# Column blocks of 512, 512 and 128 instead of 3 x 384 in the attention projections and the output projection of the last tiles

## Chip, cores and metric

One Trainium2 chip, one of its cores. The metric is the device time of one execution in microseconds (us). TensorE (PE) multiplies, VectorE (DVE) and ScalarE (ACT) work on vectors, GpSimd (POOL) does small copies and starts some of the transfers, SyncE (SP) starts the others. Each engine runs its own list of instructions in order; they meet through semaphores.

## What is computed

A two-layer encoder step for a prompt of 1024 tokens and eight samples of 16 tokens, so 1152 tokens in all, with a model width of 1024. What the change touches is, in each layer, the projection before attention and the one behind it:

```python
qa, ka, va, qb, kb, vb = split_even(h @ w_in)      # layer 0, 2304 output columns
y = jnp.concatenate([oa.reshape(b, t, A_WIDTH), ob], axis=-1) @ w_out
...
q, k, v = [z.reshape(b, t, C_HEADS, HEAD_DIM) for z in jnp.split(h @ w_in, 3, axis=-1)]   # layer 1
return o @ w_out, (k_new, v_new)
```

Around them stand a normalisation with shift and scale from a condition vector, a gated residual addition, and behind each attention a gated ConvFFN. All is float32.

## The kernel before

**Layout.** Activations lie transposed: 128 features on the partitions, 1152 tokens as columns; `h` and `hl` hold eight such feature tiles (`KT` = 8). float32 precision is had by splitting each operand into a high part (fp32r) and a low part (bf16): `mm3` (lines 84 to 88) runs three matmuls into the same accumulator, high x high, high x low and low x high, each with its own weight load.

**Stages.** `setup`, then attention "AB" (layer 0), FFN 0, attention "C" (layer 1), FFN 1, `finish`. An attention goes through tiles of 128 output features: A has tiles 0 to 3, B tiles 4 to 7, C tiles 8 to 15. For each tile a `q`, and mostly a `k` and a `v`, is needed, a *tensor* of 128 x 1152, which takes 8 weight tiles (k) times the 1152 columns. B shares a k and v between two tiles, so AB has 20 tensors and C 24.

**The column blocks.** 1152 columns don't fit in one PSUM bank (512 floats), so a tensor is made in three blocks, each over all k. `THIRDS` (line 38) makes them 384 wide. A step `("F", name, b, k)` is one `mm3` of block b (line 1520), `("P", n, b, k)` the same for the output projection of feature block n (line 1556). FFN and the very last projection use `COLS` (line 37) instead: `mm9` (lines 90 to 113) and the FFN's `first_pair` (lines 737 to 753).

**The order of work.** All engines follow one list of steps, made by `tile_steps` (line 1007) for a tile and `first_steps` (line 1067) for the first tensors. In a tile's list stand the attention's steps (`S` scores, `T` transposes of the probabilities, `V` product with the values, `N` and `O` norm and transpose of the output, `K`, `SK`, `VH`, `VI`, `PV` for the cached keys and values of the samples), and between them whole numbers, the slots: places with a weight where projection steps for the *next* tile are put as filler. A slot gets so many steps that the share of steps sent is the share of weights seen. In C with all three tensors a slot holds mostly 2 or 3 `F` steps, with up to 6 in a row near the samples' part. In the last tile of each attention (`last`), where there is no next tile, the filler is the output projection over seven of the eight feature tiles (the eighth is this tile's own output); its 8 x 3 x 7 steps stand in slots of up to 16. The seven earlier tiles' outputs have been spilled to DRAM and are read back into `h` and `hl` before it.

**Banks.** Blocks go in turn to PSUM banks 0 and 1. Block i waits (`f_free`, and line 1553 for `P`) until block i - 2 has been copied out: by ScalarE into `F[name]` for `F` (line 1786), by VectorE's `out_third` (lines 2102 to 2120) for `P`, which adds gate x product to `xT`. Columns from 1024 on are samples with a gate each, so they take two instructions of their own (lines 2115 and 2119). In `first_steps` q and k use six banks at once.

**First tensors.** `first_steps` interleaves q and k row by row of k; blocks 0 and 1 of row k run when VectorE has made row k of `hl` (`mod_dve`), block 2, which holds the samples, four rows later (`LAG`). Then v follows in three blocks, after the ring slot of q's weights has been refilled and split (`W`: ScalarE line 177, VectorE line 182).

**End.** Behind the last tile's steps `mm9` adds the product with the last feature tile, and VectorE's `residual` the result.

Of the kernel before, what the change touches and what calls it, by code (L numbers as in the profile page):

```python
# [14 lines left out]
P = 128  # L15
D = 1024
KT = D // P
SEQ = 1024
NB = 8
NS = 16  # L20
TS = NB * NS
TOK = SEQ + TS
# [12 lines left out]
IN_EVEN = 2304  # L35
THETA = 10000.0
COLS = ((0, 512), (512, 1024), (1024, TOK))
THIRDS = ((0, 384), (384, 768), (768, TOK))


C_ID = 0
# [965 lines left out]
def tile_steps(kind, T, fill, last, nxt):  # L1007


    keys = new_kv(kind, T)  # L1010
    body = []
    lead, early = (0, 0) if last else (6, 4)
    late = 0 if fill == "q" else 1
    for u in range(QB + 1):


        scored = u < QB

        one, two = ([0], [0]) if last and u < 3 else ([4], [4])
        body += [("FA", u - 1)] if u else []  # L1020
        first, second = [("S", u, 0)] if scored else [("QZ", 0)], [("S", u, 1)] if scored else []
        body += first + second + ([("V", u - 2)] if u > 1 else [])
        if u == 0:
            body += [("VT",), ("KT",), ("VS",), lead, ("KR",)] if keys else [lead]
        turned = [("T", u - 1, p) for p in range(pieces(kind, u - 1))] if u else []
        body += ([("N", u - 2)] if u > 1 else []) + one + turned[0:2]
        body += ([("O", u - 2)] if u > 1 else []) + two + turned[2:]
    body += [("LB",), ("V", QB - 1)]
    for g in range(2):
        u, x = QB + g, late if g else 1  # L1030
        body += [("K", g, 0), ("K", g, 1), 3 * x, ("N", u - 1), ("SK", g, 0), ("K", g, 2), ("O", u - 1), 2 * x,
                 ("SK", g, 1), ("K", g, 3), ("SK", g, 2), x, ("SK", g, 3), ("VH", g, 0), ("VH", g, 1), ("X", u), 9 * x,
                 ("FA", u), ("VI", g, 0), ("VI", g, 1)] + ([("QZ", 1)] if g == 0 else []) + \
                [("T", u, 0), 4 * x] + ([("CQ",) + nxt] if g and nxt else []) + \
                [("PV", g, 0), ("VH", g, 2), ("VI", g, 2), ("PV", g, 1), ("VH", g, 3),
                 ("VI", g, 3), ("PV", g, 2), x, ("PV", g, 3), ("V", u)]
    body += ([("CK",) + nxt] if nxt and new_kv(*nxt) else []) + [4 * late, ("N", QB + 1), 4 * late, ("O", QB + 1)]
    total = sum(s for s in body if isinstance(s, int))
    todo = [("P", n, b, k) for n in range(KT) for b in range(3) for k in range(KT - 1)] if last else \
        [("F", name, b, k) for name in fill for b in range(3) for k in range(KT)]  # L1040
    seen = sent = 0
    turn, later, steps = [], [], []
    for s in body:
        if not isinstance(s, int):
            steps.append(s)
            continue
        seen += s
        upto = -(-len(todo) * seen // total)
        if upto > sent or sent == len(todo):
            steps += turn  # L1050
            turn, later = later, []
        steps += todo[sent:upto]
        for f in todo[sent:upto]:
            if unit_ends(f):
                turn += [("W",)]
                later += [("R", f[1])] if f[1] in ("q", "k") else []
        sent = upto
    assert sent == len(todo)
    return steps + turn + later
# [35 lines left out]
def attention(nc, S, G, ins, outs, kinds):  # L1095
    ctx = ExitStack()
    with ctx:
# [7 lines left out]
        q, ql = sb("q", [P, TOK], F32R), sb("ql", [P, TOK], BF16)  # L1105
# [13 lines left out]
        rtmp = sb("rtmp", [P, 2, TS]) if odd else E[:, 1792:2048].rearrange("p (j t) -> p j t", j=2)  # L1119
# [10 lines left out]
        ps, h, hl, K, mb = G.psum, G.h, G.hl, G.consts, G.maskb  # L1130
# [4 lines left out]
        a = m  # L1135
        tiles, total = plan(kinds)
# [367 lines left out]
        def _(pe):  # L1504
            spread_pe(pe, S, G, m, F["v"], rs, rs_s)

            def do(what, kind, T, s, c, turns):
                n = kv(kind, T)
                first = isinstance(T, int) and T == T0
                if what == "F":  # L1510
                    nk, nT = next_tile(kind, T)
                    name, b, k = s[1:]
                    if T == T0 - 1:
                        c = cb + "qkv".index(name)
# [2 lines left out]
                        f_free(kind, T, name, b, n)  # L1517
                    if T == T0 - 1 and name != "v" and b == 0:
                        h_ready(pe, S, m, k)
                    lo, hi = THIRDS[b]  # L1520
                    mm = mm3(pe, ps[:, f_bank(T, name, b), 0:hi - lo], w[:, k * P:(k + 1) * P], wl[:, k * P:(k + 1) * P],
                             h[:, k, lo:hi], hl[:, k, lo:hi], k == 0, k == KT - 1)
                    if k == KT - 1:
# [20 lines left out]
                elif what == "P":  # L1544
                    j, b, k = s[1:]
# [7 lines left out]
                        pe.wait_ge(S.out_evac, 4 * KT * odd + i - 1)  # L1553
                    elif i == 0 and k == KT - 2:
                        pe.wait_ge(S.restored, gone + 32 * 7)
                    lo, hi = THIRDS[b]
                    mm = mm3(pe, ps[:, i % 2, 0:hi - lo], w[:, k * P:(k + 1) * P], wl[:, k * P:(k + 1) * P],
                             h[:, k, lo:hi], hl[:, k, lo:hi], k == 0, k == KT - 2)
                    if k == KT - 2:
# [3 lines left out]
                elif what == "K":  # L1563
                    g, b = s[1:]
# [9 lines left out]
                elif what == "SK":  # L1574
                    g, b = s[1:]
# [14 lines left out]
                elif what == "T":  # L1590
                    u, p = s[1:]
# [15 lines left out]
                    else:  # L1607
                        nb = width(kind, u) // P
                        for i in range(4 * p, min(4 * p + 4, nb if kind == "A" else 2 * nb)):
                            y = e_at(kind, u, i // nb) + i % nb * P  # L1610
                            mm = pe.transpose(dst[:, (i - 4 * p) * P:(i - 4 * p + 1) * P], E[:, y:y + P], ident)
                    mm.then_inc(S.turned, 1)
                elif what == "V" and s[1] < QB:
# [8 lines left out]
                    for j in range(nb):  # L1622
                        x, y = slice(j * P, (j + 1) * P), slice((k0 + j) * P, (k0 + j + 1) * P)
# [11 lines left out]
                elif what == "PV":  # L1635
                    g, b = s[1:]
# [10 lines left out]
                    for j in range(nc_):  # L1647
                        x = slice(j * all_ + b * rows, j * all_ + (b + 1) * rows)
# [101 lines left out]
        def _(act):  # L1750
# [12 lines left out]
            def do(what, kind, T, s, c, turns):  # L1763
                n = kv(kind, T)
                first = isinstance(T, int) and T == T0
                if what == "F" and s[3] == KT - 1:
                    nk, nT = next_tile(kind, T)
                    name, b = s[1:3]
                    if T == T0 - 1:
                        c = cb + "qkv".index(name)  # L1770
# [5 lines left out]
                    if T != T0 - 1 and b == 0:  # L1776
# [5 lines left out]
                            act.wait_ge(S.k_turned, n + 1)  # L1782
                        else:
                            act.wait_ge(S.v_turned, n + 1)
                    lo, hi = THIRDS[b]
                    act.copy(F[name][:, lo:hi], ps[:, f_bank(T, name, b), 0:hi - lo]).then_inc(f_sem[name], 1)
                elif what == "W":
                    split()
                elif what in ("CQ", "CK"):
                    isq = what == "CQ"  # L1790
                    kind, T = s[1:]
                    n = kv(kind, T)
# [31 lines left out]
                elif what == "T":  # L1824
                    u, p = s[1:]
# [6 lines left out]
                elif what == "K":  # L1832
                    g, b = s[1:]
# [98 lines left out]
        def _(dve):  # L1932
# [11 lines left out]
            def do(what, kind, T, s, c, turns):  # L1944
# [4 lines left out]
                elif what == "R" and not odd:  # L1949
                    rotate(s[1], *next_tile(kind, T))  # L1950
                elif what == "P" and s[3] == KT - 2:
                    out_third(s[1], s[2], c)
                elif what == "CQ":
                    dve.wait_ge(S.q_high, s[2] + 1)
                    dve.tensor_tensor(ql[:, :], F["q"][:, :], q[:, :].bitcast(F32), ALU.subtract).then_inc(S.q_low, 1)
# [143 lines left out]
                    dve.tensor_scalar(x, x, rc[:, 0:1], G.cfac[:, 0:1] if kind == "A" else None,  # L2099
                                      ALU.mult, ALU.mult if kind == "A" else ALU.bypass).then_inc(S.probs, 1)  # L2100

            def out_third(n, b, c):

                lo, hi = THIRDS[b]
                if b == 2:
                    ring.done(dve, c)
                else:
                    dve.wait_ge(S.out_ready, (3 * KT - 1) * odd + 2 * n + b + 1)
                upto = min(hi, SEQ)
                y, x = ps[:, (3 * n + b) % 2, 0:hi - lo], G.xT[:, n, lo:upto]  # L2110
                i_ = dve.scalar_tensor_tensor(out=x, in0=y[:, 0:upto - lo], scalar=G.mod[:, a, 16 + n, 0:1], in1=x,
                                              op0=ALU.mult, op1=ALU.add)
                if b == 2:
                    tmp, x = rtmp[:, n % 2, :], G.xT[:, n, SEQ:TOK]
                    ch.then(dve.tensor_tensor(tmp.rearrange("p (b q) -> p b q", b=NB),
                                              y[:, SEQ - lo:hi - lo].rearrange("p (b q) -> p b q", b=NB),
                                              G.mod[:, a, 16 + n, 1:NC9].unsqueeze(2).broadcast_to([P, NB, NS]),
                                              ALU.mult))
                    i_ = dve.tensor_tensor(x, x, tmp, ALU.add)
                i_.then_inc(S.out_evac, 1)  # L2120
# [199 lines left out]
```

## Time and profile before

| what | value |
|---|---|
| three timed runs | 3976.79, 3984.57, 3977.92 us; median 3977.92 |
| profiled execution | 3989.37 us, of which the span from first to last instruction 3987.8 us |
| granted TensorE clock, mean | 0.924 |
| PE matmuls busy | 3534.9 us |
| DVE busy | 2122.8 us |
| ACT busy | 1352.4 us |

The profile lists instructions with start and duration. A matmul's start is stamped when it may begin to enter, and its end is modelled, so durations of neighbours overlap: the pace is read from start to start. PEld are the weight loads. Names read `output<-inputs`. The granted clock is 1.00 at 2.4 GHz and 0.50 at 1.2 GHz. The FFN stages are not touched.

### The profile page before, as it was taken

Reading aid. Unit: us, or ns where it says so; the run is one execution under the profiler, and the core shown is the slowest. Engines: PE = TensorE matmul, PEld = TensorE weight load, DVE = VectorE, ACT = ScalarE, POOL = GpSimd, SP = SyncE. Lnnn points to the kernel's source line nnn. Section 1 sums busy time; section 2 is a strip of 40 time slices with the busy share of each in tenths; the row PEclk is TensorE's granted clock in tenths of the full one; section 3 lists DMA queues with packets and bytes.
Section 4 is the critical chain, followed back from the end, with each engine's and each line's share of the span. In section 5 each row is a group of like instructions: output and inputs, shape, how many; then the busy total and the mean of one; then the engine's idle time right before and its main releaser. Section 6 shows DMA issues by size and latency. Waiting matters only on the chain. (4 is left out here: it accounts for less than half of the span.)

```text
span 3987.8 us, 54257 instructions
## 1 busy us (share of the span) xinstructions
PE 3534.9 (89%) x20953; PEld 2087.5 (52%) x20953; DVE 2122.8 (53%) x3554; ACT 1352.4 (34%) x2665; POOL 485.6 (12%) x1018
## 2 busy tenths in 40 slices
PE   6878788877699999999988888888879999999997
PEld 3545455544464555555545555555546455555554
DVE  5654444455446555555555545545545655555555
ACT  6633444344223222122134444444432322212212
POOL 1012212222110000000010222211201000000000
PEclk8887888778799999999989999988989999999998
DMA  9722222211302111111111333333241211111111
GB/s 348 256 63 75 55 60 78 67 45 48 111 24 60 43 43 38 48 40 41 41 62 48 118 116 113 118 107 99 92 136 43 60 43 43 38 48 39 42 40 57
DMA packets 222127, 303.87 MB, mean 76 GB/s; under 512 B 24339, under 2 KB 174151, under 8 KB 221314
## 3 DMA queue, kind: packets, MB, share of 16 engines
q1 hardware_dynamic: 191938, 190.39, 14.7%
q0 software_dynamic: 30016, 111.15, 9.3%
q8 instruction: 112, 1.84, 0.2%
q14 instruction: 61, 0.50, 0.0%
HBM read 264.76 MB, written 63.95 MB: 82 GB/s over the span
## 5 line engine op out<-in xcount | busy, mean ns | idle before, releaser
L96 PE MATMUL psum<-h,ffn_high 128*128 128x512 f32 (+1 forms) x2016 | 989.1, 531 | 2.8 <-ACT u L858 2.8
L98 PE MATMUL psum<-hl,ffn_high 128*128 128x512 bf16 (+1 forms) x2016 | 616.2, 339 | 0.0
L100 PE MATMUL psum<-h,ffn_low 128*128 128x512 bf16 (+1 forms) x2016 | 562.9, 333 | 0.0
L96 PE MATMUL psum<-actr,ffn_high 128*128 128x512 f32 (+1 forms) x1056 | 518.1, 531 | 15.7 <-DVE actl L940 15.7
L96 PEld LDWEIGHTS psum<-h,ffn_high 128*128 128x128 f32 x2016 | 390.6, 194 | 82.9 <-ACT u L858 3.0
L98 PEld LDWEIGHTS psum<-hl,ffn_high 128*128 128x128 bf16 x2016 | 196.8, 98 | 412.8 <-issue 356.8
L86 PE MATMUL psum<-h,attC_high 128*128 128x384 f32 x744 | 365.1, 491 | 32.9 <-issue 16.5
L917 DVE TENSOR_SCALAR y<-u,cvT 128x1168 f32<-128x1168 f32 x88 | 78.2, 888 | 522.8 <-ACT u L863 522.8
L86 PE MATMUL psum<-h,attAB_high 128*128 128x384 f32 x648 | 329.4, 508 | 26.6 <-DMA hl<-act_low_dram 9.4
L98 PE MATMUL psum<-actl,ffn_high 128*128 128x512 bf16 (+1 forms) x1056 | 324.0, 340 | 0.0
L100 PE MATMUL psum<-actr,ffn_low 128*128 128x512 bf16 (+1 forms) x1056 | 295.7, 334 | 0.0
L177 ACT CAST ffn_high<-ffn_raw 128x1024 fp32r<-128x1024 f32 x132 | 139.3, 1055 | 441.4 <-PE psum L100 431.9
L857 ACT COPY u<-psum 128x1024 f32<-128x1024 f32 x88 | 89.3, 1015 | 522.5 <-PE psum L100 522.1
L87 PE MATMUL psum<-hl,attC_high 128*128 128x384 bf16 x744 | 265.1, 356 | 0.0
L88 PE MATMUL psum<-h,attC_low 128*128 128x384 bf16 x744 | 260.5, 350 | 0.0
L597 DVE SCALAR_TENSOR_TENSOR xT<-psum,mod,xT 128x1024 f32<-128x1024 f32 x192 | 245.3, 1277 | 0.0
L87 PE MATMUL psum<-hl,attAB_high 128*128 128x384 bf16 x648 | 241.0, 372 | 0.0
L88 PE MATMUL psum<-h,attAB_low 128*128 128x384 bf16 x648 | 236.4, 365 | 0.0
L96 PEld LDWEIGHTS psum<-actr,ffn_high 128*128 128x128 f32 x1056 | 205.7, 195 | 56.4 <-issue 16.7
L98 PEld LDWEIGHTS psum<-actl,ffn_high 128*128 128x128 bf16 x1056 | 103.5, 98 | 214.9 <-issue 186.0
L710 POOL COPY so<-u 128x2 f32<-128x2 f32 x88 | 18.1, 206 | 1569.7 <-ACT u L858 1569.7
L86 PEld LDWEIGHTS psum<-h,attC_high 128*128 128x128 f32 x744 | 151.9, 204 | 80.3 <-issue 40.0
(496 smaller groups left out, 7233.3 us busy)
## 6 DMA issues: line engine op xcount, KB each, us to landing
ada_raw<-in_ada_w SPq DMA_DIRECT2D x48, 1024.0 KB, 8.4
ffn_raw<-in_w_up SPq DMA_DIRECT2D x88, 512.0 KB, 3.8
ffn_raw<-in_w_down SPq DMA_DIRECT2D x44, 512.0 KB, 3.6
raw_C<-in_cache_c_k POOLq DMA_DIRECT2D x64, 256.0 KB, 3.9
raw_C<-in_cache_c_v POOLq DMA_DIRECT2D x64, 256.0 KB, 3.4
out_ck_s<-in_cache_c_k POOLq DMA_DIRECT2D x8, 1984.0 KB, 8.9
out_cv_s<-in_cache_c_v POOLq DMA_DIRECT2D x8, 1984.0 KB, 14.3
attC_raw<-in_w_in_odd SPq DMA_DIRECT2D x24, 512.0 KB, 5.6
```

The costliest lines, as they stand in the source:

```text
L86: pe.matmul(out, w, x, start=start, stop=False, skip_group_check=True)
L87: pe.matmul(out, top(w), xl, start=False, stop=False, skip_group_check=True)
L88: return pe.matmul(out, wl, top(x), start=False, stop=stop, skip_group_check=True)
L96: return pe.matmul(out, w, x[:, lo:hi], start=first and start, stop=last and stop, skip_group_check=True)
L98: return pe.matmul(out, top(w), xl[:, lo:hi], start=first and start, stop=last and stop, skip_group_check=True)
L100: return pe.matmul(out, wl, top(x[:, lo:hi]), start=first and start, stop=last and stop, skip_group_check=True)
L177: act.copy(self.w[s][:, :], self.raw[c % self.raws][:, :]).then_inc(self.high[s], 1)
L597: return dve.scalar_tensor_tensor(out=G.xT[:, n, 0:SEQ], in0=y[:, 0:SEQ], scalar=G.mod[:, a, 16 + n, 0:1], in1=G.xT[:, n, 0:SEQ], op0=ALU. ...
L710: pool.tensor_copy(so[:, 2 * g + j, 0:2], U[g][:, SEQ:SEQ + 2])
L857: act.copy(U[gate][:, 2:2 + SEQ], ps[:, 3 * gate:3 * gate + 2, :].rearrange("p b n -> p (b n)"))
L917: ch.then(dve.tensor_scalar(y[:, 0:n], u[:, 2:2 + n], cv[:, l, 2, bass.ds(f, 1)], cv[:, l, 3, bass.ds(f, 1)], ALU.mult, ALU.add))
```

## The change

`THIRDS` goes away; `F` and `P` steps and their copies use `COLS`, so blocks 0, 1 and 2 are 512, 512 and 128 columns. Block 2 now holds only the samples. `tile_steps` counts the filler in 128-column units (4, 4, 1) instead of steps: a slot takes whole steps until the columns sent reach the slot's share. `out_third` becomes `out_part`: blocks 0 and 1 have one instruction, block 2 only the two for the samples. The number of matmuls and weight loads is the same.

```diff
-THIRDS = ((0, 384), (384, 768), (768, TOK))
...
+    def columns(s):
+
+        return (COLS[s[2]][1] - COLS[s[2]][0]) // P
+
...
     seen = sent = 0
+    share = sum(columns(f) for f in todo)
     turn, later, steps = [], [], []
...
         seen += s
-        upto = -(-len(todo) * seen // total)
+        upto, due = sent, -(-share * seen // total)
+        while upto < len(todo) and sum(columns(f) for f in todo[0:upto]) < due:
+            upto += 1
...
-                    lo, hi = THIRDS[b]
+                    lo, hi = COLS[b]
                     mm = mm3(pe, ps[:, f_bank(T, name, b), 0:hi - lo], ...
...
-                    lo, hi = THIRDS[b]
+                    lo, hi = COLS[b]
                     mm = mm3(pe, ps[:, i % 2, 0:hi - lo], ...
...
-                    lo, hi = THIRDS[b]
+                    lo, hi = COLS[b]
                     act.copy(F[name][:, lo:hi], ps[:, f_bank(T, name, b), 0:hi - lo]).then_inc(f_sem[name], 1)
...
-                upto = min(hi, SEQ)
-                y, x = ps[:, (3 * n + b) % 2, 0:hi - lo], G.xT[:, n, lo:upto]
-                i_ = dve.scalar_tensor_tensor(out=x, in0=y[:, 0:upto - lo], scalar=G.mod[:, a, 16 + n, 0:1], in1=x,
-                                              op0=ALU.mult, op1=ALU.add)
-                if b == 2:
-                    tmp, x = rtmp[:, n % 2, :], G.xT[:, n, SEQ:TOK]
+                y, x = ps[:, (3 * n + b) % 2, 0:hi - lo], G.xT[:, n, lo:hi]
+                if b < 2:
+                    i_ = dve.scalar_tensor_tensor(out=x, in0=y, scalar=G.mod[:, a, 16 + n, 0:1], in1=x,
+                                                  op0=ALU.mult, op1=ALU.add)
+                else:
+                    tmp = rtmp[:, n % 2, :]
```

## Rows read from the trace of the kernel before

**Rows 1.** The page, busy time, share and instructions of each engine.

```profile
PE 3534.9 (89%) x20953; PEld 2087.5 (52%) x20953; DVE 2122.8 (53%) x3554; ACT 1352.4 (34%) x2665; POOL 485.6 (12%) x1018
```

**Rows 2.** Table of stretches of attention C: us; busy of PE, PEld, DVE, ACT, POOL; clock; DMA.

```profile
2230.00:2339.00 109.00, 94.00 (x632) 61.31 (x632) 56.75 (x131) 49.46 (x112) 22.28 (x43) 0.94 0.35 109
...
2667.00:2779.00 112.00, 98.98 (x632) 65.60 (x632) 55.93 (x129) 48.61 (x110) 22.27 (x43) 0.88 0.34 106
...
2888.00:3059.00 171.00, 146.99 (x965) 94.16 (x964) 79.49 (x179) 50.88 (x111) 19.39 (x36) 0.92 0.34 110
```

**Rows 3.** Timeline of PE (start, us long), turns of 384, 512 and 128 columns.

```profile
2098.36 0.45 PE L86 MATMUL psum<-h,attC_high 128*128 128x384 f32 x1 [0.15 <-DVE hl L560]
...
2114.55 0.48 PE L86 MATMUL psum<-h,attC_high 128*128 128x384 f32 x1
...
3113.70 0.59 PE L86 MATMUL psum<-h,ffn_high 128*128 128x512 f32 x1
...
3117.14 0.42 PE L86 MATMUL psum<-h,ffn_high 128*128 128x128 f32 x1
...
3128.84 0.31 PE L86 MATMUL psum<-h,ffn_high 128*128 128x128 f32 x1
...
3130.56 0.31 PE L86 MATMUL psum<-h,ffn_high 128*128 128x128 f32 x1
```

**Rows 4.** Table of stretches, turns of 512 and of 128 columns.

```profile
3113.70:3117.10 3.40, 3.40 (x16) 1.50 (x15) 3.37 (x4) 1.34 (x2) 0.00 (x0) 1.00 0.00 0
...
3128.80:3130.90 2.10, 2.10 (x28) 2.02 (x26) 0.00 (x0) 0.00 (x0) 0.00 (x0) 1.00 0.00 0
```

**Rows 5.** Timeline of PE at half clock, turns of 384, 512 and 128 columns.

```profile
2084.86 0.78 PE L86 MATMUL psum<-h,attC_high 128*128 128x384 f32 x1
...
2088.80 0.78 PE L86 MATMUL psum<-h,attC_high 128*128 128x384 f32 x1
...
3102.34 0.99 PE L86 MATMUL psum<-h,ffn_high 128*128 128x512 f32 x1
...
3104.95 0.99 PE L86 MATMUL psum<-h,ffn_high 128*128 128x512 f32 x1
...
308.71 0.46 PE L86 MATMUL psum<-v_AB,W_AB 128*128 128x128 f32 x1
...
309.62 0.46 PE L86 MATMUL psum<-v_AB,W_AB 128*128 128x128 f32 x1
```

**Rows 6.** Timeline of PE at the start of attention C, with the wait before.

```profile
2092.20 0.44 PE L86 MATMUL psum<-h,attC_high 128*128 128x384 f32 x1 [1.20 <-DVE hl L560]
...
2095.85 0.44 PE L86 MATMUL psum<-h,attC_high 128*128 128x384 f32 x1 [1.29 <-DVE hl L560]
...
2118.22 0.44 PE L86 MATMUL psum<-h,attC_high 128*128 128x384 f32 x1 [2.85 <-DVE attC_low L182]
```

**Rows 7.** Groups by form (count, busy, mean ns, idle before): copies and updates of C.

```profile
L1786 ACT COPY f_k_C<-psum 128x384 f32<-128x384 f32 x24 | 11.5, 477 | 5.4 <-PE psum L88 4.9
...
L1810 ACT COPY sw_C<-psum 128x128 f32<-128x128 f32 x8 | 2.1, 261 | 0.0
...
L2111 DVE SCALAR_TENSOR_TENSOR xT<-psum,mod,xT 128x384 f32<-128x384 f32 x16 | 9.9, 617 | 31.6 <-PE psum L88 31.6
...
L2111 DVE SCALAR_TENSOR_TENSOR xT<-psum,mod,xT 128x256 f32<-128x256 f32 x8 | 3.9, 483 | 16.2 <-PE psum L88 16.2
```

**Rows 8.** PE's waits (us, times, longest): seven C tiles, then four A tiles.

```profile
PE psum L86 <- DVE kcl_C L1980: 15.7, 27, 0.8
...
PE psum L116 <- DVE Wl_C L1970: 14.7, 14, 1.1
...
PE psum L1656 <- ACT osb_AB L1854: 52.1, 29, 3.0
...
PE psum L1699 <- DVE kl_AB L1958: 4.7, 1, 4.7
```

**Rows 9.** PE's waits in the last tile of C.

```profile
PE psum L96 <- DVE hl L2008: 1.5, 1, 1.5
```

More of the change, by code:

```diff
@@ L1951, in do @@
                 elif what == "P" and s[3] == KT - 2:
-                    out_third(s[1], s[2], c)
+                    out_part(s[1], s[2], c)
                 elif what == "CQ":
@@ L2100, in factors, with out_part @@
                                       ALU.mult, ALU.mult if kind == "A" else ALU.bypass).then_inc(S.probs, 1)
-            def out_third(n, b, c):
-                lo, hi = THIRDS[b]
+            def out_part(n, b, c):
+                lo, hi = COLS[b]
                 if b == 2:
@@ L2108, in out_third @@
                     dve.wait_ge(S.out_ready, (3 * KT - 1) * odd + 2 * n + b + 1)
-                upto = min(hi, SEQ)
-                y, x = ps[:, (3 * n + b) % 2, 0:hi - lo], G.xT[:, n, lo:upto]
-                i_ = dve.scalar_tensor_tensor(out=x, in0=y[:, 0:upto - lo], scalar=G.mod[:, a, 16 + n, 0:1], in1=x,
-                                              op0=ALU.mult, op1=ALU.add)
-                if b == 2:
-                    tmp, x = rtmp[:, n % 2, :], G.xT[:, n, SEQ:TOK]
+                y, x = ps[:, (3 * n + b) % 2, 0:hi - lo], G.xT[:, n, lo:hi]
[4 more added lines that the diff above has]
+                    tmp = rtmp[:, n % 2, :]
                     ch.then(dve.tensor_tensor(tmp.rearrange("p (b q) -> p b q", b=NB),
-                                              y[:, SEQ - lo:hi - lo].rearrange("p (b q) -> p b q", b=NB),
+                                              y.rearrange("p (b q) -> p b q", b=NB),
                                               G.mod[:, a, 16 + n, 1:NC9].unsqueeze(2).broadcast_to([P, NB, NS]),
```

## The prediction

> **What bounds the kernel now.** I read the page first, for the share of each engine, then a table of stretches, then the tensor engine's timeline in a few short windows, then its waits. Two words are used below: a *turn* is the three matmuls of one `mm3` call, and a *k-turn* is one weight tile against all 1152 columns, three turns in either kernel.
>
> TensorE is the busiest engine, 89% of the span [rows 1]. In the attention stages that the change touches it is not always full: a tile of C takes 109 us with 94 us of matmul, and the last one with the output projection of C 171 us with 147 [rows 2]. The projection turns of the next tile are the filler between the attention's own steps. Where TensorE waits right after a filler slot, a longer slot costs nothing; elsewhere it costs its full length.
>
> **Cost of one k-turn.** 384-column turns run back to back from 2098.36 to 2114.55 us, 31 intervals: 0.522 us each, 0.523 between most. The first pair of the FFN runs the shapes of the change: 512-column turns from 3113.70 to 3117.14, five intervals, 0.688 us; 128-column turns from 3128.84 to 3130.56, seven intervals, 0.246 us [rows 3]. So a k-turn costs 3 x 0.523 = 1.569 us before and 2 x 0.688 + 0.246 = 1.622 us after: **+0.053 us**. The reason can be read: from 384 to 512 columns a turn grows by 0.165 us per 128, so 0.523 would fall to 0.194 at 128 columns, but it is 0.246. In the stretch of 128-column turns weight loads are busy 2.02 of 2.10 us, in that of 512 only 1.50 of 3.40 [rows 4]. Three weight loads no longer fit behind three short matmuls. At half clock the same turns take 0.985 (2084.86 to 2088.80, four), 1.305 (3102.34 to 3104.95, two) and 0.455 us (308.71 to 309.62, two) [rows 5], which makes +0.11 per k-turn.
>
> The page "TensorE: Matmul & The Clock Gate" of the Trainium skill, section "Back-to-back issue gap", gives the isolated gap as columns over 2.4 GHz plus 2.5 ns; by that alone nine matmuls over 1152 columns cost the same however they are cut, the k-turn difference would be 0, and the sum below -4 us where the rows give +13. Its own warning that at small N this leaves out the weight loads, with 81 ns per matmul at N=128, is an estimate of 0.243 us per turn and agrees with the 0.246 measured; its 131 ns for N=512 does not agree with 0.229 here. The rows decide.
>
> There are 44 projection tensors of 8 k-turns and 16 output blocks (8 in each attention) of 7: 352 + 112 = 464 k-turns, so **+24.6 us** if every one lay on the path at full clock. Now by place.
>
> **Start of each attention (6 of the 44 tensors).** q and k run together, paced at first by VectorE's `hl`; blocks 0 and 1 of row k go ahead, block 2 follows four rows later. The waits are 1.29 us before row 3 [rows 6] and 0.15 before row 4, and none after [rows 3]. With blocks of 512 more work lies in the early, waiting rows: row 3 starts at 2095.85 and takes 4 x 0.688 = 2.75, so row 4 starts at 2098.60 rather than 2098.36. Then four rows of 4 x 0.688 + 2 x 0.246 = 3.24 us and a tail of 8 x 0.246 = 1.97: end at 2113.5. Before, 32 turns of 0.523 end at 2115.1. Gain 1.6. The first two rows run at half clock and are longer, but the 1.20 us wait before row 2 and the 1.29 before row 3 [rows 6] take up to about 2.5 of that. The 2.85 us wait before v [rows 6] holds ScalarE's copy of k's last block, which falls from 0.48 (384 columns) to 0.26 (128) [rows 7]: another 0.2. v costs +0.42, in AB hidden by the 4.7 us wait for `kl` [rows 8]. Sum for both attentions: -1.8 and -1.4, **-3.2 us**.
>
> **The 38 tensors inside tiles.** Each is 8 x 0.053 = +0.42 us, all of it in its block 2. By the order of steps, q's block 2 falls behind `O` of unit 1 and `N` of unit 2, k's into the section of the cached keys, v's at the tile's very end, with nothing after it but the next scores. In C the waits that could take it up are those for `kcl` (15.7 us, 27 times) and for `Wl` before the values (14.7 us, 14 times), in seven tiles [rows 8]: short, under 1.1 us each, a few per tile. I take 0.9 of the 1.26 us per tile: **+6.3** in C. In A the transposes of the normed output wait 52.1 us, 29 times [rows 8], and take all of q's and half of k's: 0.6 a tile for four tiles, **+2.5**. The B tiles load five tensors: **+1.4**. Bounds: 38 x 0.42 = 16.0, or 38 x 0.86 = 33 were all at half clock, against 0.
>
> **The slots.** The planner now counts columns. A slot of two or three turns of 384 (6 or 9 units of 128 columns, 1.05 or 1.57 us) becomes one or two turns of 512 (4 or 8 units, 0.69 or 1.38 us). The total is unchanged, the distribution coarser. In a C tile the slots just before a wait grow (between the pieces of `T` of unit 4, after `T` of units 8 and 9: two units each), which costs nothing; the slot before `T` of unit 5 falls from 9 to 4, and the two single turns in the cached-key and value sections go to 0 or 1. If those shrunk slots open no new wait the change gains 4 units, 0.7 us a tile; if each becomes a wait it loses up to 1.5. Nearest is that most do, since the steps behind them already wait (up to 0.8 and 1.1 us [rows 8]): I take +0.2 a tile, **+1.4** in C, 0 elsewhere.
>
> **Output projection.** 16 x 7 x 0.053 = **+5.9**; these slots are the long ones and almost nothing waits behind them. VectorE's three updates (0.617, 0.617 and 0.483 plus two small ones [rows 7]) become two and the two small ones. By the slope of the two rows a 512-column update is about 0.75 us. Only the last of each stage is on the path: the final matmuls wait 1.5 us for `hl` [rows 9], queued behind block 2's update; it loses the 0.48 us piece: **-1.0** for both. The other updates lie beside matmuls, VectorE waiting 31.6 and 16.2 us for them [rows 7]. If that cover went, each would cost its 0.75.
>
> DMAs: none is added or moved by more than a slot. ScalarE keeps three copies a tensor; same columns.
>
> Sum: -3.2 + 6.3 + 2.5 + 1.4 + 1.4 + 5.9 - 1.0 = **+13.3 us**. The profiled execution took 3989.37 us (span 3987.8), 0.3% above the median of 3977.92; it would become 4002.7. Carried to the median: **3991.2 us**.
>
> **Rivals.**
> *The fillers hide it.* All 38 tile tensors and slots vanish in waits: -3.2 + 5.9 - 1.0 = +1.7, 3979.6. For it: TensorE waits in every tile. Against: the waits are short and not behind v's block. 0.20.
>
> *No extra cost of short turns*, if weight loads run ahead while other steps stand between them: -3.2 - 1.0, 3973.7. Against it stands the measured 0.246. 0.04. (This is what the simple gap rule of the Trainium skill's page cited above would give.)
>
> *Faster, through the clock.* Slots before the waits of A, 1.8 us each in the mean [rows 8], grow from 6 to 8 units, which takes 0.33 off, and TensorE falls less often to 1.2 GHz. Two C tiles with the same work took 109 us at a granted 0.94 and 112 at 0.88 [rows 2], 0.5 us per 0.01. If fourteen tiles gain 0.03, that is -21 and the sum -8: 3970. It decides from 0.02 a tile, where it cancels the loss. Against: other slots shrink by 5 units and make new idle time. 0.12.
>
> *Slower, through the banks.* After block 2 the next block 0 needs block 1's bank; the cover falls from 7 x 0.523 = 3.7 us to 7 x 0.246 = 1.7, and an update takes 0.75. If VectorE or ScalarE is over a microsecond late there, one wait of about 1 us for each of 16 blocks gives 4007. Against: VectorE waits for TensorE there, not the reverse. 0.07.
>
> **The numbers.** 0.57 is left for the forecast. Its own range is 3980 to 4000. The low end for 8 in 10 takes in the hidden case and part of the clock's, 3972; the high end has every tile tensor on the path (+10 more) and a few microseconds of clock: 4005. A measurement can tell some 0.2% (8 us) from no change. Slower by more: nearly all of the forecast and the banks, 0.61. Same: hidden, no cost, and the forecast's low tail, 0.27. Faster: 0.12.
>
> **What would show it.** Right: L86 to L88 in groups of 512 and 128 columns, dense 128-column turns at 0.246 with weight loads near full; v of the first tensors starting some 1.8 us earlier; C tiles near 110 us; the output stages 2 to 3 us longer. Wrong: C tiles at 109 or below with waits gone; a granted clock that moved by more than 0.01; waits of L86 for VectorE's updates of `xT` or for ScalarE's copies at L1786.

## The result and the profile after

| | before | after |
|---|---|---|
| median of 20 runs beside each other, us | 3979.81 (3976.31 to 3992.83) | 3992.9 (3975.99 to 4005.3) |
| ratio, 95% interval | | 1.003 [1.002, 1.004] |
| profiled execution, us (span) | 3989.37 (3987.8) | 3994.59 (3993.0) |

The change costs 13.1 us. The two profiled executions are only 5.2 us apart, since that of before was itself 0.2% above the median of its 20 runs. So medians say what a change costs, and traces say where, with a scatter of their own that has to be measured too (below).

The page of after, the line that answers to [rows 1]:

```profile
PE 3560.4 (89%) x20953; PEld 2076.3 (52%) x20953; DVE 2122.1 (53%) x3538; ACT 1351.0 (34%) x2665; POOL 485.3 (12%) x1018
```

TensorE has the same number of matmuls and is busy 25.5 us more. VectorE has lost its 16 extra updates. The stretches that answer to [rows 2], two C tiles and the last one (columns as there):

```profile
2210.00:2320.00 110.00, 97.08 (x632) 62.60 (x632) 56.66 (x132) 49.13 (x111) 22.18 (x43) 0.91 0.34 107
2642.00:2751.00 109.00, 95.82 (x632) 62.11 (x632) 56.39 (x131) 49.13 (x111) 22.18 (x43) 0.92 0.34 109
2886.00:3063.00 177.00, 155.47 (x961) 94.40 (x959) 77.42 (x166) 51.34 (x112) 19.29 (x36) 0.87 0.32 106
```

The tiles take 109 and 110 us, against 109 and 112. The last one takes 177 instead of 171, at a granted clock of 0.87 instead of 0.92: in attention C the loss is in the output stage, not in the tiles. VectorE's updates and ScalarE's copies by form, answering to [rows 7]:

```profile
L2118 DVE SCALAR_TENSOR_TENSOR xT<-psum,mod,xT 128x512 f32<-128x512 f32 x16 | 12.0, 750 | 25.9 <-PE psum L87 25.6
...
L1793 ACT COPY f_k_C<-psum 128x128 f32<-128x128 f32 x8 | 2.1, 266 | 2.1 <-PE psum L87 2.1
```

The 512-column update takes the 0.75 us that was estimated, the copy of k's last block 0.27.

### The profile page after: what moved, and what is told of

Same layout as the page of the kernel before. It is cut to its first block and busy times, and to the rows that moved or that the text cites. A ratio compares the mean times of both kernels' runs of the same rounds, so it can differ in the third digit from the quotient of the medians.

```text
span 3993.0 us, 54241 instructions
## 1 busy us (share of the span) xinstructions
PE 3560.4 (89%) x20953; PEld 2076.3 (52%) x20953; DVE 2122.1 (53%) x3538; ACT 1351.0 (34%) x2665; POOL 485.3 (12%) x1018
## 5 line engine op out<-in xcount | busy, mean ns | idle before, releaser
L85 PE MATMUL psum<-h,attC_high 128*128 128x512 f32 (+1 forms) x744 | 366.6, 506 | 25.3 <-issue 10.2
L85 PE MATMUL psum<-h,attAB_high 128*128 128x512 f32 (+1 forms) x648 | 333.8, 527 | 24.9 <-DMA hl<-act_low_dram 9.5
L86 PE MATMUL psum<-hl,attC_high 128*128 128x512 bf16 (+1 forms) x744 | 267.8, 360 | 0.0
L87 PE MATMUL psum<-h,attC_low 128*128 128x512 bf16 (+1 forms) x744 | 261.7, 353 | 0.0
L86 PE MATMUL psum<-hl,attAB_high 128*128 128x512 bf16 (+1 forms) x648 | 244.6, 377 | 0.0
L87 PE MATMUL psum<-h,attAB_low 128*128 128x512 bf16 (+1 forms) x648 | 238.1, 369 | 0.0
```

The lines of the kernel that those rows point to most:

```text
L85: pe.matmul(out, w, x, start=start, stop=False, skip_group_check=True)
L86: pe.matmul(out, top(w), xl, start=False, stop=False, skip_group_check=True)
L87: return pe.matmul(out, wl, top(x), start=False, stop=stop, skip_group_check=True)
```

## A yardstick from fourteen traces

The experiments use one kernel in which the block widths of q, k, v (FBLOCKS below) and of the output projection (PBLOCKS), and the weights by which the planner fills its slots, are set apart. The weights follow the widths unless a diff says otherwise; where a block crosses the boundary between text and samples, its update has both parts. Where the stretches begin and end is read from the same instructions in each trace: the tiles run from ScalarE's first copy of `v` (first tile) to its copy of `q` (last tile of B) or `v` (last tile of C), and the output ends with the first matmul that spreads the next normalisation's factors (`spread_pe`). In us:

| kernel | start AB | AB tiles | last B, output | FFN0 and start C | seven C tiles | last C, output |
|---|---|---|---|---|---|---|
| before | 57.2 | 772.1 | 167.2 | 938.4 | 763.9 | 192.2 |
| e4_null | 57.6 | 774.3 | 166.5 | 938.4 | 761.5 | 190.5 |
| e3_p448 | 57.5 | 764.9 | 167.6 | 938.3 | 760.6 | 196.2 |
| e1_p_only | 57.4 | 771.7 | 170.9 | 938.4 | 761.6 | 196.8 |
| e5_p_defer | 57.8 | 771.8 | 168.4 | 939.6 | 758.7 | 195.4 |
| e6_p_slots | 57.7 | 767.6 | 169.2 | 938.1 | 761.7 | 197.6 |
| e7_p_even | 57.6 | 765.5 | 169.9 | 938.3 | 762.9 | 190.9 |
| e10_null_wait | 57.8 | 774.5 | 170.0 | 938.1 | 759.2 | 194.9 |
| e8_first_only | 56.2 | 765.9 | 166.6 | 936.5 | 760.1 | 191.1 |
| e2_f_only | 55.6 | 772.1 | 167.0 | 936.7 | 761.0 | 187.3 |
| after | 55.9 | 779.0 | 171.3 | 936.3 | 756.5 | 199.4 |
| e9_after_defer | 56.1 | 775.4 | 168.6 | 938.3 | 757.2 | 195.4 |
| e12_f448 | 56.5 | 785.3 | 166.6 | 934.7 | 761.0 | 191.9 |
| e11_f_slots | 57.7 | 784.2 | 167.2 | 938.2 | 784.9 | 192.7 |

The first nine have the same tiles, and their AB tiles still scatter over 764.9 to 774.5, the C tiles over 758.7 to 763.9. A difference of a few us between two traces means nothing there. The start of AB and the last B tile repeat within about 1 us in kernels that are alike there, and there a single trace can be read. The last C tile does not: among the six kernels with output blocks of 384 and even slots (before, e4, e8, e2, e12, e11) it takes 187.3 to 192.7.

The scatter of the AB tiles goes in part with TensorE's clock: it was granted 0.824 to 0.843 of full speed in the nine, 0.843 in e7_p_even (765.5 us) and 0.824 in e4_null (774.3 us).

## The experiments

The diffs are shortened: a table of blocks is written by its widths, and `weights` stands for the list that the planner counts by. The line with the minus is the changed kernel for e1, e2, e8 and e9, e1_p_only (q, k, v in 3 x 384) for e3 to e7, and e4_null for e10 to e12.

**1. Undo one half of the change each.** The output projection alone, and q, k, v alone:

```diff
# e1_p_only
-FBLOCKS = 512, 512, 128
+FBLOCKS = 384, 384, 384
# e2_f_only
-PBLOCKS = 512, 512, 128
+PBLOCKS = 384, 384, 384
```

> Only the output projection of the two last tiles in blocks of 512, 512 and 128; all q, k, v tensors as before in 3 x 384. Theory A (short turns are held up by their weight loads, 0.053 us per k-turn, minus VectorE's last piece): 16 x 0.37 - 1.0 = +4.9 us. Theory B (the projection stages also lose full clock, as the trace of the changed kernel shows for its last C stage, 178 us at a granted 0.88 instead of 171 at 0.92): +10 to +14 us. Both have the dense 128-column turns at 0.246 us.

> Only the q, k, v tensors in blocks of 512, 512 and 128, slots by columns; the output projection as before in 3 x 384. Theory A as predicted: 13.3 - 4.9 = +8.4 us, C tiles 1.1 us longer each. Theory B (read from the one trace of the changed kernel: start -3, AB tiles +4, C tiles -7): -6 us, C tiles 1 us shorter each. If B holds, the whole loss is in the output projection.

Measured: output projection alone 3992.61 (3984.5 to 3993.41, six runs) against 3979.52, ratio 1.0033 [1.0020, 1.0046]; q, k, v alone 3982.13, 1.0013 [1.0002, 1.0023]. So 112 of the 464 k-turns, a quarter, carry nearly all of the loss. The first lies in the range of theory B, the second (+2.6) between the two theories (+8.4 and -6) and in neither.

**2. Output projection without short turns, and the generated kernel itself.**

```diff
# e3_p448
-PBLOCKS = 512, 512, 128
+PBLOCKS = 448, 448, 256
# e4_null
-PBLOCKS = 512, 512, 128
+PBLOCKS = 384, 384, 384
```

> Only the output projection in blocks of 448, 448 and 256 columns. Theory A: a turn of 256 columns is long enough for its loads (0.358 us by the slope, against 0.246 of loads), a k-turn costs 2 x 0.605 + 0.358 = 1.568 us as before, so 0 to -0.3 us. If unequal blocks cost by themselves (coarser slots, a shorter cover for the bank, the clock) it is slower by 2 us or more all the same.

> The kernel before once more, its blocks written through tables of 3 x 384. Both theories: 0 us, within 1.5. Its profile is a second look at the kernel before, to tell what differs from run to run in the length of the stages and in the granted clock: I expect stages to differ by up to 2 us.

Measured: 3980.93, ratio 1.0004 [0.9996, 1.0013], and 3980.53, 1.0003 [0.9992, 1.0015]. Neither can be told from before. 256-column blocks are free, as the weight loads let expect, but that says only that the cost comes with the 512/512/128 form: it has short turns, and it also ends its blocks at other places.

**Reading the trace of e1_p_only against that of e4_null, slot by slot.** Three consecutive slots of the output stage (from 1084.79) hold 6, 5 and 10 turns and last 4.23, 3.63 and 3.83 us to the next step, 11.69 together; the same three in e4_null (from 1088.36) hold 7 each and last 3.75, 3.84 and 3.75, 11.34. That is +0.35 for the 21 turns of one output block, where 0.37 was costed (7 x 0.053). Then, in both attentions, a wait of 1.1 us that e4_null does not have. In C it is

```profile
PE psum L1619 <- DVE E_C L2112: 1.1, 1, 1.1
```

Unit 9 is the second of the samples' two units, the last of a tile; `FA` is the step in which VectorE works out a unit's softmax factors (`factors`), and block (6, 1) is column block 1 of feature block 6. VectorE's timeline in e1_p_only just there in AB (start, us long, idle before):

```profile
1150.41 0.75 DVE L2125 SCALAR_TENSOR_TENSOR xT<-psum,mod,xT 128x512 f32<-128x512 f32 x1 [4.10 <-PE psum L90]
1151.08 0.15 DVE L2094 TENSOR_TENSOR st_AB<-st_AB 128x1 f32<-128x1 f32 x1
1151.26 0.16 DVE L2102 RECIPROCAL st_AB<-st_AB 128x1 f32<-128x1 f32 x1
1151.46 0.35 DVE L2112 TENSOR_SCALAR E_AB<-E_AB,st_AB 128x256 f32<-128x256 f32 x1
```

and TensorE's, the last filler turn ahead of the transposes of unit 9, and these:

```profile
1150.52 0.23 PE L89 MATMUL psum<-hl,attAB_high 128*128 128x128 bf16 x1
1150.59 0.22 PE L90 MATMUL psum<-h,attAB_low 128*128 128x128 bf16 x1
1151.87 0.44 PE L1619 MATMUL psum<-consts,E_AB 128*128 128x128 f32 x2 [1.06 <-DVE E_AB L2112]
```

VectorE was idle for 4.10 us, with the update of block (6, 1) next in its program and the factors of unit 9 behind it. That block is complete only at 1150.4, two short turns (0.5 us) before the slot ends. TensorE then waits for the update plus three small operations. In e4_null the same update starts earlier against the transposes:

```profile
1150.03 0.62 DVE L2125 SCALAR_TENSOR_TENSOR xT<-psum,mod,xT 128x384 f32<-128x384 f32 x1 [3.05 <-PE psum L90]
1150.56 0.15 DVE L2094 TENSOR_TENSOR st_AB<-st_AB 128x1 f32<-128x1 f32 x1
1150.75 0.16 DVE L2102 RECIPROCAL st_AB<-st_AB 128x1 f32<-128x1 f32 x1
1150.94 0.35 DVE L2112 TENSOR_SCALAR E_AB<-E_AB,st_AB 128x256 f32<-128x256 f32 x1
```

and TensorE's transposes follow at

```profile
1152.97 0.38 PE L1619 MATMUL psum<-consts,E_AB 128*128 128x128 f32 x2
```

There six turns of 384 stand behind the block (140 of the 168 turns end with it, and the slot ends after 146, against 142 in e1_p_only), 2.9 us from the update's start to the transposes, and the factors are there 1.7 us early (1151.29 against 1152.97).

**3. Take the queue away, change the slots, keep the slots.** The first kernel keeps every block and slot of e1_p_only and only swaps two things on VectorE:

```diff
# e5_p_defer
+                elif what == "P" and s[3] == KT - 2 and s[1:3] == (6, 1):
+                    pass
...
                 elif what == "FA":
                     factors(kind, T, s[1])
+                    if T == TL and s[1] == QB + 1:
+                        out_part(6, 1, c)
# e6_p_slots: blocks of 384, weights of the planner
-        PBLOCKS = 512, 512, 128; weights 4, 4, 1
+        PBLOCKS = 384, 384, 384; weights 4, 4, 1
# e7_p_even: blocks of 512, 512, 128, weights of the planner
-        weights 4, 4, 1
+        weights 1, 1, 1
# e8_first_only: 512, 512, 128 only in the steps of first_steps
-FBLOCKS = PBLOCKS = 512, 512, 128
+FBLOCKS = PBLOCKS = 384, 384, 384
```

> As the kernel with the output projection alone in 512/512/128 (median 3992.61), but VectorE works out the factors of unit 9 before it adds the block (6, 1), instead of behind it. In that kernel TensorE waits 1.06 us for them before the transposes of unit 9, in each of the two output stages, and half-clock stretches follow. Theory queue: the wait goes, -2.1 us for both, and some of the half-clock stretches behind it with it, -3 to -6 more: 3984 to 3988, and no wait of L1619 for the probabilities of unit 9. Theory turns: the short turns set the cost and the wait was only idle time that would have come anywhere: 3991 to 3993, the wait turns up at another step. Theory clock by chance: the wait goes, the half-clock stretches stay: 3990 to 3991.

> All blocks stay 3 x 384; only the slots of the output projection are filled as if its blocks weighed 4, 4 and 1, so 6, 5 and 10 turns of 0.52 us in turn instead of 7, 7, 7, and 13 and 9 about unit 9. No short turns. Theory turns: 0, 3980 (within 2 us of the kernel before). Theory slots (uneven slots open waits that the even ones did not have): +5 to +9, 3985 to 3989, with new waits of TensorE in both output stages.

> Output projection in 512/512/128, its slots counted by turns as before (7 each), so a slot is 4.82, 4.82 or 1.72 us long. The block (6, 1) ends 1.5 us ahead of the factors of unit 9, so they are not queued. Theory turns: +5.9 - 1.0 and the same clock loss as with counted columns, 3985 at least, 3992 if the rest of the +13 belongs to the short turns too. Theory queue: without the 1.06 us waits, 3984 to 3987. Against either: every third slot has 1.9 us less work than before, and may leave waits of its own, +1 us for each of up to 7 slots in each stage: 3998.

> Only the first tensors q, k, v of each attention (6 of 44) in 512/512/128, everything else 3 x 384. The prediction gave them -3.2 us (-1.8 and -1.4): 3976.5, and a start of the AB attention 1.8 us shorter. By the traces so far the AB start gives 1.6 to 2.0 and the C start 0.1 to 0.2: 3977.5 to 3978.5. Rival: the time gained there is given back later in the stage (the next steps wait for the same loads or caches): 3980.

Measured, against 3980.77 for before:

| | median, us (12 runs) | ratio |
|---|---|---|
| e5_p_defer | 3980.95 (3973.08 to 3992.7) | 1.0002 [0.999, 1.0014] |
| e6_p_slots | 3983.94 (3976.94 to 3992.02) | 1.0006 [0.9995, 1.0017] |
| e7_p_even | 3990.24 (3971.61 to 3996.58) | 1.0021 [1.0009, 1.0034] |
| e8_first_only | 3976.74 (3965.19 to 3984.75) | 0.9992 [0.9977, 1.0007] |

Moving one VectorE instruction behind three others takes the output projection from +13 (six runs) to nothing that can be told from zero, more than the theory that proposed it had asked for (3984 to 3988). VectorE's timeline in e5_p_defer:

```profile
1151.37 0.75 DVE L2129 SCALAR_TENSOR_TENSOR xT<-psum,mod,xT 128x512 f32<-128x512 f32 x1 [3.45 <-PE psum L90]
1152.03 0.48 DVE L1997 TENSOR_TENSOR kcl_AB<-raw_AB,kc_AB 128x128 bf16<-128x128 f32 x2
```

and TensorE's, where the transposes show no wait:

```profile
1151.60 0.39 PE L1619 MATMUL psum<-consts,E_AB 128*128 128x128 f32 x2
1151.74 0.31 PE L88 MATMUL psum<-h,attAB_high 128*128 128x128 f32 x1
...
1151.99 0.31 PE L88 MATMUL psum<-h,attAB_high 128*128 128x128 f32 x1
...
1152.23 0.31 PE L88 MATMUL psum<-h,attAB_high 128*128 128x128 f32 x1
```

VectorE's work before the update, the factors among it, ended at 1147.92 (1151.37 less 3.45), and nobody waits for the update. The short turns are as slow as before, 0.245 us from start to start. So they are not what cost 13 us. The swap was not put into the kernel before; that it would gain nothing there is not shown.

The uneven slots alone (e6) cost about 3, not separated from 0 and between its two theories, with the last B tile 2 us longer. They too leave only two turns behind block (6, 1), but of 0.52 us, and the transposes of unit 9 wait 0.3 us in each attention instead of 1.1. e7 is a counterexample to a simple story: no update stands before unit 9 at the wrong time, no short wait shows up, yet it costs 9.5 us. By its counts and the durations of [rows 3] its slots of seven turns last 4.82, 4.82 and 1.72 us where they had 3.66 each, so it has an unevenness of its own. Its last B tile takes 169.9 us, 3 more than with 384, without any wait at unit 9, so an output stage can get longer without the queue. It measured in the range of theory turns and outside that of theory queue. Where it loses was not found: its profiled execution (span 3980.0 us) lay 9 us below its median.

**4. The cross tests.** The same swap in the changed kernel; the same wait put into the kernel before; and the tiles' slots and blocks apart.

```diff
# e9_after_defer: the swap of e5_p_defer, all blocks 512, 512, 128
# e10_null_wait: all blocks 384
                 elif what == "FA":
+                    if T == TL and s[1] == QB + 1:
+                        for _ in range(9):
+                            ch.then(dve.tensor_tensor(rtmp[:, 1, :], rtmp[:, 1, :], rtmp[:, 1, :], ALU.max))
                     factors(kind, T, s[1])
# e11_f_slots: all blocks 384, weights of F
-        weights 1, 1, 1
+        weights 4, 4, 1
# e12_f448: weights 7, 7, 4
-FBLOCKS = 384, 384, 384
+FBLOCKS = 448, 448, 256
```

> The changed kernel (512/512/128 everywhere, median 3992.9) with the one difference that VectorE works out the factors of unit 9 before it adds block (6, 1). With the output projection alone this took 3992.61 to 3980.95, of which the two waits by themselves are 2.1 us. Theory queue and clock (the wait sets off half-clock stretches): again -8 or more, 3980 to 3986, what is left being the tile tensors. Theory wait alone (the rest of the -11.7 was scatter of the runs, six of one kernel against twelve of the other): -2.1, 3990 to 3991.5.

> The kernel before (3 x 384 everywhere) with nine idle VectorE operations of about 0.3 us put ahead of the factors of unit 9 in the last tile of each attention, so that TensorE waits there about 1 us as in the changed kernel, with no short turn anywhere. Theory wait alone: +2 us for the two, 3982 to 3983. Theory queue and clock: +8 to +12, 3988 to 3992, with more half-clock stretches behind the wait. If the other steps of VectorE that are held up too (the new W of the cached values) open waits, 2 to 3 us on top under either.

> All blocks 3 x 384 and the output projection as before; only the slots of the 38 tensors inside tiles are filled as if blocks weighed 4, 4 and 1. No short turns, no change at the start. q, k, v in 512/512/128 without the output projection took 3982.13, of these tensors the first six alone 3976.74: so the 38 others and their slots cost +5.4. Theory turns (0.42 us a tensor less what waits take): 3980 to 3981, no change. Theory slots (coarser slots open waits): 3983 to 3986.

> q, k, v (first ones and those in tiles) in 448/448/256, output projection 3 x 384. In the output projection blocks of 256 columns cost nothing (3980.93). Theory turns: the 38 tile tensors cost nothing, the first six keep the part of the gain that comes from more work in the early rows: -1 to -2 us, 3978.5 to 3979.5. Theory slots (a coarser slot costs whatever the turn): +2 to +5, 3982 to 3985. It would beat both kernels only if it comes below 3978.

Measured, against 3979.86 for before:

| | median, us (runs) | ratio |
|---|---|---|
| e9_after_defer | 3985.78 (12) | 1.0007 [0.9996, 1.0019] |
| e10_null_wait | 3987.63 (12) | 1.0017 [1.0002, 1.0033] |
| e11_f_slots | 4017.96 (6) | 1.0079 [1.0059, 1.0099] |
| e12_f448 | 3987.52 (12) | 1.0013 [1.0001, 1.0025] |

The swap takes 7.1 us from the changed kernel (3992.9 to 3985.78), and the same wait with no short turn anywhere adds 7.1 to e4_null (3980.53 to 3987.63) and 7.8 to the kernel before. VectorE's timeline in e10_null_wait (in AB the scratch tile `rtmp` lies in `E`, so the nine inserted operations read `E_AB`):

```profile
1148.53 2.89 DVE L1987 TENSOR_TENSOR E_AB<-E_AB 128x128 f32<-128x128 f32 x9
...
1151.85 0.35 DVE L2115 TENSOR_SCALAR E_AB<-E_AB,st_AB 128x256 f32<-128x256 f32 x1
```

and TensorE's wait (us, times, longest):

```profile
PE psum L1619 <- DVE E_AB L2115: 1.2, 1, 1.2
```

Two waits of 1.2 us cost 7 by the medians, three times their length. By this run alone that is not sure: the interval begins at 1.0002, 0.8 us, and 2.4 lies inside. The three pairs together say it: by means, e1 less e5 is 9.2 us, after less e9 6.8, e10 less e4 6.3, each good to about 2; their average is 7.4, and resampling the runs gives 4.9 to 9.8.

Does a lower clock make up the rest? The end of attention AB and the start of the FFN, 35 us from about the same point of the stage (columns as in [rows 2]), in e4_null:

```profile
1180.00:1215.00 35.00, 25.58 (x115) 17.61 (x114) 23.27 (x27) 12.66 (x13) 0.53 (x1) 0.71 0.29 76
```

in e1_p_only:

```profile
1180.00:1215.00 35.00, 25.59 (x109) 18.39 (x108) 21.72 (x25) 11.95 (x12) 0.52 (x1) 0.66 0.28 76
```

in e5_p_defer:

```profile
1180.00:1215.00 35.00, 25.60 (x115) 17.44 (x114) 23.09 (x27) 13.04 (x14) 0.52 (x1) 0.71 0.29 76
```

in e10_null_wait:

```profile
1180.00:1215.00 35.00, 25.58 (x113) 18.09 (x113) 22.05 (x26) 12.08 (x13) 0.53 (x1) 0.66 0.28 76
```

in the kernel after:

```profile
1185.00:1220.00 35.00, 25.58 (x107) 18.00 (x107) 21.97 (x26) 11.95 (x12) 0.52 (x1) 0.62 0.28 76
```

and in e2_f_only, which has no such wait:

```profile
1173.00:1208.00 35.00, 25.58 (x115) 18.18 (x114) 22.34 (x26) 11.95 (x12) 0.53 (x1) 0.66 0.28 76
```

The three with the wait have the lower clock, but it does not go with the wait. With the window laid at the same point of the stage in all fourteen traces (from 19 us before the first matmul of `spread_pe` to 16 behind it), five have 0.71 (before, e3, e4, e5, e9), eight 0.66 and after 0.61 (0.62 a microsecond earlier, above); six of the eight, e2, e6, e7, e8, e11 and e12, have no wait of 1 us there. The lower clock costs about 1 us there, with or without the wait.

The last B tile in the yardstick says as much: 166.5 to 167.6 us with blocks of 384 in even slots or of 448 and no such wait, 168.4 and 168.6 with the 512/512/128 projection and no queue, 170.9 and 171.3 with the queue, 170.0 with the inserted wait; but also 169.2 in e6 and 169.9 in e7.

The runs on record tell a little more, since each has its granted clock. Within one kernel a run with 0.001 more of it is 1.9 us shorter (244 runs, correlation -0.70), which goes with about half of the variance. In the three pairs the slower kernel has the lower mean clock: 0.9232 against 0.9258, 0.9232 against 0.9241, 0.9239 against 0.9243. By that slope the clock goes with 2.5 us of the 7.4; the delay at the transposes, 1.3 us an attention in the traces, is 2.6. Whether the wait lowers the clock, or the runs happened to fall so, is not shown.

e11_f_slots, the largest effect of the study, has no other block than the kernel before. Its seven C tiles take 784.9 instead of 761.5. TensorE's waits over them, e4_null:

```profile
PE psum L1619 <- DVE E_C L2112: 18.2, 14, 2.1
...
PE psum L1624 <- DVE Wl_C L1983: 13.1, 7, 1.9
PE psum L1624 <- ACT sw_C L1832: 6.9, 4, 2.5
```

and e11_f_slots:

```profile
PE psum L1619 <- DVE E_C L2112: 29.2, 14, 3.1
...
PE psum L1624 <- DVE Wl_C L1983: 15.9, 16, 1.7
PE psum L1624 <- ACT sw_C L1832: 12.7, 7, 4.1
```

These three grow by 19.6 of the 23.4 us. With 384-column turns counted 4, 4, 1 many slots shrink to one or two turns (0.5 or 1.0 us) where a softmax chain needs cover, and others grow to six (3.1 us). Its 4017.96 us lie far above both theories (3980 to 3986). In the changed kernel the same counts go with turns of those sizes, the time per slot stays near even, and the C tiles are no longer than before. So counts that do not fit the widths cost some 23 us in C alone. The reverse for these tiles, blocks of 512, 512 and 128 counted by turns, was not run.

e12_f448 cost 7.7 us where 0 or a gain was expected from the turns; it lies above both theories, nearer to that of slots (2 to 5), and its AB tiles took 785.3 us, outside the 764.9 to 774.5 of the nine. Its waits for `osb` and `kcl` in AB are longer (53.8 and 40.7 us against 48.2 and 35.5 in e4_null), at a granted clock of 0.82 in both. One trace; which slot does it was not tried.

## Why the prediction was right, and where its sum was not

The forecast of 3991.2 us came within 2 us of 3992.9, and slower was the likely case. The forecast's +13.3 stands against a measured +13.1. The total is right, though, with the parts wrong in both directions: that they cancelled is luck.

| term | predicted | by medians | in the traces |
|---|---|---|---|
| starts of the attentions | -3.2 | -4.0 (e8) | AB -1.6 (57.6 to 56.0), C -1.6 (last section) |
| 38 tensors in tiles and their slots | +6.3 + 2.5 + 1.4 + 1.4 = +11.6 | +5.4 (e2 less e8) | C -2.9 (761.1 to 758.2), AB +5.7 (769.8 to 775.5) |
| output projection, turns and last update | +4.9 | +0.2 (e5) | last B +1.6 (166.9 to 168.5), last C +4.5 (190.9 to 195.4), near its scatter |
| queue on VectorE before unit 9 | 0 | +11.7 (e1 less e5), +7.1 (after less e9), +7.1 (e10) | last B +2.6, last C +1.4 and +4.0 |

Means over the nine kernels with tiles of 384 and the three of 512 are used for the tiles. A median of twelve runs that spread over 20 us is good to about 2 us, so each middle entry is to some 2 or 3, and neither the -4.0 nor the +0.2 can be told from zero. The 11.7 rests on six runs of e1.

**The turns.** Right as a mechanism: 512-column updates took 0.750 us, 128-column turns 0.245, three slots 0.35 us more where 0.37 was costed. Eight output blocks are then 2.8 us a stage, but the last B tile grew by 1.6 and the median of e5 by 0.2; what takes up the rest was not traced beyond the last wait for `hl`, which fell from 1.5 us [rows 9] to 1.1 rather than by 0.48. The gap rule of the Trainium skill ("TensorE: Matmul & The Clock Gate", "Back-to-back issue gap") would have made this term zero; the 0.35 us and the 0.245 speak against using it at 128 columns.

**The start.** Right: -1.8 was forecast for AB, -1.6 measured. In C -1.4 was forecast and -1.6 measured, once starts with a like granted clock are compared: 51.9 to 52.0 us in the four kernels with the new start, 53.6 in the six with the old one (last section).

**The tiles.** Over-sized. The 0.42 us of each tensor was laid on the path for seven tenths in C ("I take 0.9 of the 1.26 us per tile"), and the C tiles came out 3 us shorter instead of 7.7 longer, though that is near their scatter. The rival "the fillers hide it" was right for C. For AB it stays open: the three are 5.7 us longer in the mean, at a granted clock of 0.831, 0.822 and 0.823 where the nine had 0.824 to 0.843. The medians (e2 less e8) leave +5.4 for all 38. The slots term had the wrong size by its form: slots are worth 20 us and more, not 1.4, when time and count part (e11); here they do not.

**The output projection.** The step that failed is "these slots are the long ones and almost nothing waits behind them". TensorE's next step did wait: not for its own queue but for VectorE's, on which the update of a finished block stands ahead of the factors. The prediction had even priced the update (0.75 us, "if that cover went") and the banks rival had a wait of about 1 us from it, but at a bank and for each of 16 blocks. It is one place in each attention, for softmax factors, and two such waits cost more than their length (7.4 us in the mean of three pairs, 2.6 as delay at the transposes). To find it one would have had to lay the new ends of blocks over VectorE's program: list the slots with the planner's new counts, mark each block's last turn, and ask which VectorE step follows and how soon TensorE wants its result. Six turns of 0.523 us behind the block became two of 0.245.

**A correct total from two errors.** 6 us too much in the tiles and 7 too little in the output stages cancelled. The experiment that changed only one half showed it at once; the total alone would have confirmed a wrong account.

**What stays open.** Where all of the 7 to 12 us come from when two waits of 1.1 us go. The delay at the transposes is 1.3 us an attention, and some 2.5 us of the average of 7.4 go with the granted clock of the runs; the rest, 2 to 3 us, is as large as the error. The traces of e1 and e5 differ by 3.3 us in all. Why e7_p_even is slow without the queue. No version clearly beats the kernel before: e8_first_only was lowest, 3976.74, with an interval that holds 1.

## What to carry to other kernels

When work that fills gaps is cut anew, its cost per instruction is the small part. Look at where each piece now *ends*: what another engine does on that end stands in front of whatever comes next in its program, and the engine that fed it may want that next thing. Count filler in time, not in pieces: here a count that did not fit cost 23 us in seven tiles.

Split a change with several parts by experiment even when the total comes out as forecast. And before reading a stage in two traces, learn from unchanged stages how far they scatter.

## What the runs showed of the hardware

A wait of 1.2 us, put in twice in 3980 us by nine idle VectorE operations each, made the kernel 7.8 us slower than the runs of before beside it (ratio 1.0017 [1.0002, 1.0033]). Together with the two kernels from which such waits were taken away, the cost of two is 7.4 us in the mean (4.9 to 9.8).

Identical instructions take 1.6 us more or less by where a stretch of half clock falls. The FFN between the attentions, from that matmul of `spread_pe` to the first of C's q, takes 886.1 to 886.4 us in five traces (before, e3, e4, e5, e9) and 884.3 to 884.9 in nine. The five were granted half clock for a short stretch about 42 us in, the nine were not. In e4_null and in e1_p_only there (columns as in [rows 2]):

```profile
1239.00:1246.00 7.00, 6.02 (x26) 3.17 (x27) 5.83 (x6) 5.38 (x9) 1.75 (x5) 0.76 0.03 7
...
1240.00:1247.00 7.00, 5.83 (x34) 3.23 (x34) 5.67 (x5) 5.58 (x10) 1.75 (x5) 1.00 0.03 7
```

The start of C behind it, up to ScalarE's first copy of `v`, shows the same. With the old start it takes 52.0 us in three traces and 53.6 in the six that have such a stretch in it; the four with the new start all have one and take 51.9 to 52.0, and e12_f448 has none and takes 50.4. In before and in e1_p_only there:

```profile
2118.00:2125.00 7.00, 6.78 (x40) 4.01 (x40) 2.03 (x3) 1.53 (x2) 0.00 (x0) 1.00 0.53 152
...
2118.00:2125.00 7.00, 5.46 (x22) 3.05 (x22) 2.36 (x2) 1.09 (x2) 0.00 (x0) 0.76 0.53 151
```

So two traces of one stage are compared only beside its granted clock.
